# Modulation pieces of the pool stages are issued from GpSimd's queue instead of SyncE's

## The reference, cut to what matters

```
cond = silu(c)                                   # c: 2048 numbers
for i in (0, 1):
    mod = cond @ mod_w[i] + mod_b[i]             # mod_w[i]: 2048 x 6144
    shift, scale, gate = split(mod, 3)
    h = rms_norm(x, norm_g[i]) * (1 + scale) + shift
    out = pool_branch(h, ...) if i == 0 else dsa_branch(h, ...)
    x = x + gate * out

def pool_branch(h, w_in, w_grp, layer_scale, w_out):
    v, gate = split(h @ w_in, 2)                 # w_in: 2048 x 4096
    pooled = sliding means of v minus v          # windows 2, 4, 8, 16
    mixed = per group: pooled @ w_grp[g]         # 4 of 512 x 512
    return (mixed * layer_scale * silu(gate)) @ w_out    # w_out: 2048 x 2048
```

## Time and profile before

| | us |
|---|---|
| median of 3 executions | 2426.16 |
| the profiled execution's own time | 2423.46 |
| its span, first to last instruction | 2421.7 |
| PE busy | 2346.1 (97%) |
| DVE busy | 1545.3 (64%) |
| ACT busy | 1116.3 (46%) |
| POOL busy | 15.2 (1%) |

### The profile page before, as it was taken

How to read it: one execution, slowest core, us unless ns; L and a number is a source line. 1 busy time by engine, 2 the same in 40 slices (tenths; PEclk the granted TensorE clock), 3 DMA queues, 4 the chain that set the end, 5 groups by cost and what they waited for, 6 DMA issues and landing times.

```text
span 2421.7 us, 31105 instructions
## 1 busy us (share of the span) xinstructions
PE 2346.1 (97%) x10938; PEld 1896.5 (78%) x10938; DVE 1545.3 (64%) x1863; ACT 1116.3 (46%) x1339; POOL 15.2 (1%) x21
## 2 busy tenths in 40 slices
PE   5999999999999989999998999998999999999997
PEld 1877777788778768888787888887888888888886
DVE  1988897666696566875765444665565555555555
ACT  1454445444444445545444444444544444444444
POOL 0000000000000000000000000000000000000000
PEclk9999999999999999999999999999999999999999
DMA  9999996555697436756454766555556655655652
GB/s 394 376 376 383 376 400 222 166 176 181 214 374 245 139 144 195 226 159 190 129 176 138 235 193 193 181 195 182 165 187 193 193 185 190 191 188 189 192 185 104
DMA packets 245062, 527.95 MB, mean 218 GB/s; under 512 B 20956, under 2 KB 21220, under 8 KB 241000
## 3 DMA queue, kind: packets, MB, share of 16 engines
q1 hardware_dynamic: 241376, 510.40, 62.7%
q0 software_dynamic: 1936, 13.67, 1.5%
q10 hardware_dynamic: 1656, 2.65, 0.3%
HBM read 520.35 MB, written 6.30 MB: 217 GB/s over the span
## 4 chain that ended last, share of the span: by engine, by line
PE 90%; DVE 5%; DMA 2%; issue 2%; ACT 1%; DVEq 0%; ACTq 0%; SPq 0%
PE ps L1852 28%; PE ps L1854 28%; PE ps L1853 28%; PE ps L1921 2%; DMA T<-in_mod_w 2%; DVE wide L1257 1%; PE ps L1951 1%; DVE w_lo L1018 0%; PE ps L2124 0%; DVE tmp L1474 0%; ACT tmp L802 0%; PE ps L2022 0%; PE ps L2097 0%; DVE stage L1496 0%; PE ps L2145 0%
## 5 line engine op out<-in xcount | busy, mean ns | idle before, releaser
L1018 DVE TENSOR_TENSOR w_lo<-raw,w_hi 128x1024 fp32r<-128x1024 f32 x784 | 945.0, 1217 | 487.9 <-ACT w_hi L513 470.7
L513 ACT CAST w_hi<-raw 128x1024 fp32r<-128x1024 f32 x784 | 814.5, 1047 | 857.3 <-PE ps L1854 784.4
L1852 PE MATMUL ps<-w_hi,xa_hi 128*128 128x512 f32 x2176 | 855.7, 393 | 10.2 <-DVE w_lo L1018 3.7
L1854 PE MATMUL ps<-w_hi,xa_lo 128*128 128x512 f32 x2176 | 848.1, 390 | 0.0
L1853 PE MATMUL ps<-w_lo,xa_hi 128*128 128x512 f32 x2176 | 847.6, 390 | 0.0
L1852 PEld LDWEIGHTS ps<-w_hi,xa_hi 128*128 128x128 f32 x2176 | 409.1, 188 | 106.8 <-issue 12.9
L1854 PEld LDWEIGHTS ps<-w_hi,xa_lo 128*128 128x128 f32 x2176 | 408.9, 188 | 86.0
L1853 PEld LDWEIGHTS ps<-w_lo,xa_hi 128*128 128x128 f32 x2176 | 409.2, 188 | 82.3
L1852 PE MATMUL ps<-w_hi,xb_hi 128*128 128x512 f32 x928 | 366.2, 395 | 2.9 <-DVEq L1498 1.4
L1854 PE MATMUL ps<-w_hi,xb_lo 128*128 128x512 f32 x928 | 362.2, 390 | 0.0
L1853 PE MATMUL ps<-w_lo,xb_hi 128*128 128x512 f32 x928 | 362.1, 390 | 0.0
(11 more groups left out here) (259 smaller groups left out, 978.2 us busy)
## 6 DMA issues: line engine op xcount, KB each, us to landing
raw<-in_w_in SPq DMA_DIRECT2D x176, 512.0 KB, 4.2
T<-in_mod_w SPq DMA_DIRECT2D x160, 512.0 KB, 7.8
raw<-in_attn_w_in SPq DMA_DIRECT2D x144, 512.0 KB, 4.5
raw<-in_w_up SPq DMA_DIRECT2D x128, 512.0 KB, 4.5
raw<-in_w_down SPq DMA_DIRECT2D x128, 512.0 KB, 4.2
raw<-in_pool_w_in SPq DMA_DIRECT2D x64, 512.0 KB, 8.2
T<-in_mod_w SPq DMA_DIRECT2D x16, 1024.0 KB, 8.9
raw<-in_pool_w_out SPq DMA_DIRECT2D x32, 512.0 KB, 8.2
```

What stands on the lines that cost most here:

```text
L513: nc.scalar.copy(w_hi[:, o % SPL, :, 0:cols], raw[:, o % RAW, :, 0:cols]).then_inc(hi_ready, 1)
L1018: tt(w_lo[:, o % SPL, :, part], raw[:, o % RAW, :, part], w_hi[:, o % SPL, :, part].bitcast(F32), ALU.subtract).then_inc(lo_ready, 1)
L1852: mm(dst, x_hi, h, start=first and k == 0, stop=False)
L1854: ins = mm(dst, x_lo, h, start=False, stop=last and k == KPC - 1)
```

## The change

The two helpers `ride_first` and `ride_pe`, and the loops that call them, move from the program of SP to the program of POOL. Each keeps its wait and its transfer. On POOL they stand in a loop over the chunks of the pool stages, at the chunk whose progress they wait for, that is at the index minus 8. `clear(3)` moves into that loop, to the chunk behind the one in which PE uses piece 20. The riders of units 0, 2 and 3 count on semaphores of their own, `ride_in`; unit 5, which stays on SP, keeps `ride_landed`, counted from zero.

```diff
+        ride_in = [sem(f"ride_in{i}") for i in range(4)]
...
@@ SyncE's loop over the pool stages
                         load(SOURCES[name], b, j, B0 + b, first=g < RAW)
-                        for q in range(len(RIDE_CHUNK)):
-                            if g == (RAW - 1, RAW - 1, RAW + 2, RAW + 4)[q] if q < 4 else g == RIDE_CHUNK[q - 4] + RAW:
-                                ride_first(q)
-                        for q in range(len(PE_CHUNK)):
-                            if g == PE_ISSUE[q]:
-                                ride_pe(q)
...
@@ GpSimd's program
             clear(0)
-            pool.wait_ge(mod_taken, KC + PE_LAST + 1)
-            clear(3)
+            def ride_first(q):
+                pool.wait_ge(*((mod_used, q - 3) if q >= 4 else (tp_ready, JOBS["norm0"] + q + 1)))
+                pool.dma_start(ride_raw[:, q % 4:q % 4 + 1, :], piece(RIDE_UNIT[q // 32], 0, q % 32)
+                               ).then_inc(ride_in[q % 4], 16)
+            def ride_pe(q):
...
+                pool.dma_start(pe_raw[s].unsqueeze(1), piece(4, 0, q)).then_inc(pe_landed[s], 16)
+            for q in range(4):
+                ride_first(q)
+            for chunk in range(PHASES["idx_q"][0] * CPB):
+                if chunk == PE_CHUNK[PE_LAST] + 1:
+                    pool.wait_ge(mod_taken, KC + PE_LAST + 1)
+                    clear(3)
+                for q in range(4, len(RIDE_CHUNK)):
+                    if RIDE_CHUNK[q - 4] == chunk:
+                        ride_first(q)
+                for q in range(len(PE_CHUNK)):
+                    if chunk == PE_ISSUE[q] - RAW:
+                        ride_pe(q)
             pool.wait_ge(combined, 4)
...
@@ rider, on VectorE
-                dve.wait_ge(ride_landed[o % 4], lap * 16)
+                if u in RIDE_UNIT:
+                    dve.wait_ge(ride_in[o % 4], lap * 16)
+                else:
+                    dve.wait_ge(ride_landed[o % 4], (lap - RIDE[u] // 4) * 16)
```

More of the change, by code:

```diff
@@ L321, in src_branch, with piece @@
             return w[:, KPC * k:KPC * k + KPC, bass.ds(b * NBLK, NBLK)]
+        mws = [mod_w[i].rearrange("(p k) (u n) -> p u k n", k=KC, n=D) for i in range(2)]
+        def piece(u, b, j):
+            return mws[u // 3][:, u % 3, bass.ds(b * 4 + j // 2, 1), j % 2 * 1024:j % 2 * 1024 + 1024]
         up = plain(w_up_2[0], 0)
@@ L365, in load_phase @@
                                 ride(u, b, j)
-            mws = [mod_w[i].rearrange("(p k) (u n) -> p u k n", k=KC, n=D) for i in range(2)]
             sp.dma_start(csil[:], c[0].rearrange("(p k) -> p k", k=KC)).then_inc(c_landed, 16)
@@ L373, in _ @@
                 sp.dma_start(mod_raw[:, k % 4, :], mws[0][:, 1, k, :]).then_inc(mod_landed[k % 4], 16)
-            def piece(u, b, j):
-                return mws[u // 3][:, u % 3, bass.ds(b * 4 + j // 2, 1), j % 2 * 1024:j % 2 * 1024 + 1024]
             def ride(u, b, j):
@@ L381, in ride @@
                 sp.dma_start(ride_raw[:, j % 4:j % 4 + 1, :], piece(u, b, j)).then_inc(ride_landed[j % 4], 16)
[L383 to L400, removed]
             for name in ("pool_v", "group", "pool_gate", "pool_out", "idx_q"):
@@ L475, in _ @@
             clear(0)
-            pool.wait_ge(mod_taken, KC + PE_LAST + 1)
-            clear(3)
+            def ride_first(q):
[3 more added lines that the diff above has]
+            def ride_pe(q):
+                s = PE_SLOT[q]
+                if PE_PREV[q] is not None:
+                    pool.wait_ge(mod_taken, KC + PE_PREV[q] + 1)
+                if PE_PREV[q] is None and s < 2:
+                    pool.wait_ge(tp_ready, JOBS["pool_v"] + 4)
+                if PE_PREV[q] is None and s in (2, 3):
+                    pool.wait_ge(sum_rows, 1)
+                if s >= 4 and q >= 4 and PE_PREV[q] < 4:
+                    pool.wait_ge(staged, STAGED["group"] + 4)
+                pool.dma_start(pe_raw[s].unsqueeze(1), piece(4, 0, q)).then_inc(pe_landed[s], 16)
[11 more added lines that the diff above has]
+                        ride_pe(q)
             pool.wait_ge(combined, 4)
```

## The result

| | before | after |
|---|---|---|
| median, us (13 runs each) | 2425.23 | 2430.77 |
| lowest to highest, us | 2420.96 to 2427.03 | 2427.64 to 2433.25 |
| the profiled execution, us | 2423.46 | 2433.25 |
| its span, us | 2421.7 | 2431.5 |

The ratio is 1.0024, with a 95% interval of 1.0016 to 1.0031: the change costs some 5.5 us. That lies within the range of 2423 to 2436, but the forecast was 2426 us, no change, with 0.73 for it, and that is wrong. The range was drawn that wide for another failure (late riders in the first stage), so that the time falls in it is luck.

The account below looks back on a forecast made before the run. PE was taken to bound the pool stages, hardly stopping from 72 to 387 us. The terms summed to 0, with bounds of -0.4 and +2 us, so 2426 us on the scale of the runs shown; the range was 2423 to 2436.

Parts of the forecast that it names:

- `clear(3)` term: `clear(3)` in POOL's loop: rider 65 lands at 296.6, 1.3 us late, once; worth 0, perhaps 2 us at worst.
- the lead covers it: At `clear(3)`: DVE was 1.70 us late there before and PE stood full, so rider 65's lateness costs 0.
- What the change does to landing times: Riders on q0 land 6.8 us after issue instead of 7.5; weight chunks bear the rest out of 9 us.
- the 9 us of slack: Weight chunks in the pool stages: about 9 us early before ACT takes them, so later loads cost nothing.
- The packets taken in turn: Both queues full: engines alternate packets, a rider's 4 KB against a chunk's 2 KB, so riders get about two thirds.
- The first rival (late riders): First stage: riders landing later than 8.7 us on average slow PE; 2436 us at 10, 2445 at 11.2; chance 0.15.
- The second rival (shared port): Pool stages: DVE stands still during POOL's DMA issues, 11 us late in the first, another 13 in the last; about 2450; chance 0.06.
- Faster: Pool stages: PE's pace could hide small stalls; the profile names 0.4 us, even 4 us gives 2422; chance 0.06.

Follow-up runs that it names:

- `split_first`: The changed kernel, but DVE makes `xb_lo` of this one job before rider 67 instead of after it; median 2424.74 us, ratio to before 1.0003.
- `clear_behind`: The changed kernel with `clear(3)` moved on POOL behind riders 65 and 66, four PE pieces still ahead of rider 67; median 2426.39 us, ratio to before 1.0005.
- `two_ahead`: The changed kernel with two of the four PE pieces left ahead of rider 67, two issued later; median 2425.38 us, ratio to before 1.0001.

## Why the prediction was wrong

**The step that failed is the `clear(3)` term**, which was put at 0, and in it three things. It was costed as 1.3 us late, once, for rider 65 alone. Rider 65 did come about as computed (295.3 us, computed 296.6) and cost PE nothing. But the text itself says that rider 66 and four PE pieces stand behind `clear(3)` as well, and never asks when rider 67, behind them all, lands: 5.2 us later than before, 2.8 of it from the hold. Second, it took 6.8 us for any rider. That held for spaced riders in the first stage, where weight chunks used to stand between them. In a row of modulation pieces the old queue brought one every 1.3 us, the new queue one every 2.05, which makes the other 2.5 us; rider 67 took 13.8 us. Third, "the lead covers it" was not worked out for anything that stands behind a rider on DVE: the deadline was `xb_lo`, with 1.16 us, as `split_first` shows. The upper bound of the term, 2 us that would pass through, missed it as well: it is 4.04 us of idle PE and 6.63 with the clock in the profiled execution, some 5.5 us in the medians.

**What the change does to landing times was right.** In the first stage riders from POOL landed after a median of 6.6 us (forecast 6.8, before 7.5), weight chunks after 9.1 instead of 7.3 (the prediction had used the riders' 7.5 for them as well):

```profile
T<-in_mod_w POOLq DMA_DIRECT2D x28, 512.0 KB, 6.6
raw<-in_pool_w_in SPq DMA_DIRECT2D x20, 512.0 KB, 9.1
```

ACT never waited for such a chunk in the pool stages, so the 9 us of slack held. Riders 0 and 1 landed at 64.1 and 66.2 us (forecast about 65). q0 carried 80.78 MB, 67 more; POOL was busy for 82.8 us (forecast some 85).

**The packets taken in turn were right**, and they slow the burst. From 294 to 307 us the two queues were both full:

```profile
q0 software_dynamic: 912, 3.31, 66.9%
q1 hardware_dynamic: 808, 1.57, 34.0%
```

Nearly as many packets each, twice the bytes for q0: 3.31 MB in 13 us is 255 GB/s, and 0.52 MB then takes 2.05 us. In the kernel before the one queue had 399 GB/s from 289 to 301 us, hence some 1.3 us for the same piece. This is the cost of a shared pair of queues: q0 favours riders over weight chunks, but within q0 a rider behind four pieces waits longer than it did in q1. On this the Trainium skill (DMA: Bandwidth & Descriptors, Issuing engines are not separate DMA queues) says that DMAs from different engines interleave on the same 16 engines and that a second issuer saves only the sequencer's time. The trace agrees as far as it goes: both queues together moved 376 GB/s from 294 to 307 us, the one queue before 396, so the second queue brought no more bytes.

**The first rival (late riders)** had the right kind of failure and the wrong place and size: it asked for an average over 8.7 us in the first stage, where nothing happened (PE full, chunk 6 with 0.21 us of margin against 0.15). What came was one rider, 13.8 us, in the last stage, where the modulation pieces issued from 290 to 302 us had a median of 12.5 us, against 10.3 before. An average over a stage was the wrong question.

**The second rival (shared port) is false here:** with 128 issues on POOL between them, `lo` takes 1224 ns and a rider 1278 ns in the median, 1225 and 1279 before. No run here shows whether DVE's copies and POOL's issues hold each other up. The riders' row after:

```profile
L1267 DVE SCALAR_TENSOR_TENSOR T<-T,csil x64: 1276/1278/1285, 71.7 to 384.5; 128x1024 f32<-128x1024 f32 x64
```

**Faster** was held unlikely, rightly: in the profile before, PE had nothing to give back, and no version is faster.

**Also wrong:** DVE's wait for riders was to fall below 5.8 us and rose to 10.0, of which rider 67 has 6.5; without it it is 3.5.

**Left open:** how large the half-clock share is in a typical execution. The losses in the stretch and the rises of the medians stand in the same order (0.88 and 0.6, 1.18 and 1.3, 4.22 and 1.6, 4.62 and 4.3, 6.63 and 5.5, 7.23 and 8.4 us), but `clear_behind` with 4.22 and 1.6 is far off. Each loss is read from one execution, and a median carries an interval of 2 to 3.5 us to either side.

## What to carry to other kernels

When issues move to another engine, write out the old and the new order of the whole queue around each wait in it, with the bytes that each transfer finds ahead of it and the rate that the queue will have: a wait at the head turns spaced issues into a burst, an early transfer in the burst delays a late one behind it, and a burst that had one full queue for itself takes longer when another full queue shares the engines. Then ask of the consumer what comes next in its own order, and take the tightest deadline there; here it was not the repeated instruction whose lead I had measured but a single one behind it with 1.16 us. On an engine that is full, count a stall at more than its length: here the clock fell in each stall of 2.35 us and more, or just behind it.

## What the runs showed of the hardware

- A PE idle for 4.04 us was followed by some 5 us of multiplying at the lower clock level and so cost 6.63 us; 2.73 us of idle time cost 4.62, 2.35 cost 4.22. In `two_ahead` 0.58 us cost 0.88 with the granted clock at 1.00 throughout (304 to 315 us). So part of the cost of a stall on PE lies behind the stall.
- With two full queues, q0 and q1 got 912 and 808 packets of unequal size, 3.31 and 1.57 MB. The shares of the bandwidth went by packet size. A row of 512 KB pieces landed 2.05 us apart in the shared state and 1.3 us apart with one queue alone.
- POOL took 0.53 us for each issue of 512 KB, and q0's riders landed sooner (6.6 us) than SP's had (7.5 us), at the cost of the weight chunks.
